# More filler products before the first sums, one fold moved behind a chunk's products, and mask additions moved from VectorE to GpSimd

## The chip, the core and the metric

The kernel runs on one core of one Trainium2 chip. The metric is device time in microseconds (us) from one launch, the median of several runs. The engines are written as in the profile: PE is TensorE's matmul side and PEld its weight loads, DVE is VectorE, ACT is ScalarE, POOL is GpSimd, SP is SyncE, which starts most DMAs. An "ACT table load" is ScalarE fetching another set of functions.

## The reference

Two transformer blocks run one after the other on 256 tokens of width 1024, with 256 context tokens beside them in the first block. What matters here is the first block, which has two layers:

```python
for l in range(DEPTH):                      # DEPTH = 2
    mod_x = silu(c) @ w_ada[l] + b_ada[l]   # nine shifts, scales and gates of 1024
    mod_c = silu(c_ctx) @ w_ada[l] + b_ada[l]
    h  = h  + 0.5*g1 *swiglu(modulate(rms_norm(h),  sh1, sc1), w_gate, w_up, w_down)
    hc = hc + 0.5*cg1*swiglu(modulate(rms_norm(hc), csh1, csc1), w_gate, w_up, w_down)
    p = modulate(rms_norm(h), shm, scm) @ w_in[l]
    ...                                     # window, global and neighbourhood attention
    h = h + gm * (concat(y_w, y_g, y_n) @ w_out[l])
    h = h + 0.5*g2*swiglu(modulate(rms_norm(h), sh2, sc2), w_gate2, w_up2, w_down2)
```

In neighbourhood attention a query sees 4 rows of 16 columns around its own column, with a learned bias for each offset. The kernel scores all 256 keys instead and adds one table to the scores: the learned bias, and a large negative number where a key lies outside the 16 columns. That large negative number is the mask of this change.

## The kernel before

Every product in float32 is made of three matmuls of split operands: each operand is a high part (`..._hi`) and a low part (`..._lo`), and high times high, high times low and low times high are added up in a PSUM bank. ACT makes the high parts with a copy, DVE the low parts with a subtraction. Activations are kept with features on the 128 partitions, in eight chunks `h[:, j, :]` of 512 tokens (256 of x, 256 of the context). The weights come as a stream of panels that SP loads; PE works through them in order. The order on each engine is the order in which the Python program writes its instructions, with semaphores between engines (`Engine.after` waits, `Engine.do` signals).

The opening makes the first norm, the first two shift and scale rows of `mod`, and the first two panels of the first gate and up products at the same time:

- ACT squares the eight chunks and DVE adds them up (L996, L1004). Meanwhile PE runs products of `csil` (silu of the two conditions, 32 columns wide) whose result in bank 0 is never read (L1039): the unread products. Behind them stand the sums over the features by a column of ones (L1054).
- `ada_columns(j)` (L885) multiplies `csil` with the eighth j of the shift and scale columns, on four column groups of PE side by side. `ada_copy(j)` (L898, DVE) copies the result to SBUF, `ada_fold(j)` (L904, PE) adds the four groups up and turns the rows into columns, and `ada_scale(j)` (L913 and L916, DVE) adds the bias. These give chunk j its shift and scale. `columns_begin(j)` is the first two, `columns_end(j)` the last two.
- `norm_scale` spreads the inverse norms over the partitions (L1079, PE). `chunk_hi(j)` multiplies chunk j by them (L1443, DVE), applies scale and shift and makes the high part (L1447, L1450, ACT). `chunk_lo(j)` makes the low part (L1455, DVE). `weights_hi` and `weights_lo` split the weights (L1417, L1427).
- `products(panel, j)` are the matmuls of chunk j (L1488 with the high part of the chunk, L1492 with the low part).

The loop in `opening` writes this for chunk after chunk: while PE multiplies chunk k, DVE and ACT make chunk k+1, and PE takes the columns and the fold for chunk k+2 between `products(0, k)` and the next `products(0, k+1)`.

For the attention of layer l, POOL loads the bias table `nbr` with 12 DMAs as soon as the down panels of the first feed-forward are far enough (L1595). In the phase `in`, which makes queries, keys and values, the norm comes first, and the weight tiles then run between the steps of attention units: a generator `program` gives out weight tiles as filler, and a unit's steps are scores (L1919, PE), `exponentials` (a mask for window heads L1941, a maximum L1942, DVE; L1956, ACT), `normalise` (L1969, L1972, DVE), transposes (L1986, PE), a copy (L1993, ACT), and products with the values (L2008, PE). `turn` is the rotation of queries and keys, whose DVE steps are L1783, L1784 and L1786. After weight tile 8, `nbr_masks` adds the mask to the six heads of `nbr` on DVE (L1796). Neighbourhood units come late in the order, so `nbr` is read late.

In the second layer POOL also loads `vec_2` and the positions behind the bias table, and from the end of the attention on it builds a bias map for the second block in small steps (`bias_map`, L1389 to L1395).

Of the kernel before, what the change touches and what calls it, by code (L numbers as in the profile page):

```python
# [22 lines left out]
P = 128  # L23
# [13 lines left out]
NBR_COLS = 64  # L37
NBR_DR = 2 * NBR_ROWS - 1
# [702 lines left out]
def build(nc, ins, out):  # L741
# [6 lines left out]
    pe, act, dve = e.T, e.A, e.V  # L748
# [41 lines left out]
    def cst(name, width=P, k=0):  # L790
        o = CC.at[name] + k
        if o >= CC.kept:
            return tables[0][:, o - tables[1]:o - tables[1] + width]
        return const[:, o:o + width]
# [38 lines left out]
    loaded = [(s_vec, 16), (s_const, 16)] + [(s, 16) for s in s_tok]  # L833
# [7 lines left out]
    pool = e.G  # L841
# [9 lines left out]
    for l in range(L1):  # L851
        for hh in range(6):
            o = (l * 6 + hh) * NBR_DR
# [181 lines left out]
    dve.after((s_vec, 16))  # L1035
    pe.after((s_vec, 16), c_ready)
    csil_row = csil[:, :, :].rearrange("p k c -> p (k c)")
    for _ in range(9):
        pe.q.matmul(banks[0][0:32, 0:S], csil[:, 0, :], csil_row, start=True, stop=True)  # L1039

    split_u = {}
# [50 lines left out]
    def root_table(function=ACT.Sqrt):  # L1092

        act.do(act.q.activation(root_warm[:, :], cst("eps", 1), function))
# [304 lines left out]
    def opening():  # L1399
# [9 lines left out]
        def columns_end(j):  # L1409

            ada_fold(j)
            scaled_by[j] = ada_scale(j)
# [65 lines left out]
        def products(panel, j):  # L1478

            high, low = chunk[j]  # L1480
            pe.after(weights[j])
            by_stream = j == 0 and panel == 0
            for s in range(2 if by_stream else 1):
                pe.after(high[s] if by_stream else high)
                cols = slice(s * S, s * S + S) if by_stream else slice(0, T)
                for b in range(2):
                    for w in (first_hi, first_lo):
                        pe.q.matmul(banks[2 * panel + b][:, cols], w[:, panel, j, b * P:b * P + P], u_hi[:, j, cols],  # L1488
                                    start=j == 0 and s == 0 and w is first_hi, stop=False)
            pe.after(low)  # L1490
            for b in range(2):
                r = pe.q.matmul(banks[2 * panel + b][:, :], first_hi[:, panel, j, b * P:b * P + P], u_lo[:, j, :],  # L1492
                                start=False, stop=j == KC - 1)
            if j == KC - 1:
                r.then_inc(st.s_pe, 1)
# [14 lines left out]
        weights_lo(1)  # L1510
        columns_begin(2)
        chunk_lo(1)
        columns_end(2)
        weights_hi(2)
        for k in range(1, KC):
            if k == 3:
                root_table(ACT.Silu)
            if k + 1 < KC:
                chunk_hi(k + 1)
                weights_lo(k + 1)  # L1520
                chunk_lo(k + 1)
            if k + 2 < KC:
                weights_hi(k + 2)
            products(0, k)
            if k + 2 < KC:
                columns_begin(k + 2)
            products(1, k - 1)
            if k + 2 < KC:
                columns_end(k + 2)
            if k in (5, 6):  # L1530
                for quarter in (2 * k - 10, 2 * k - 9):
                    st.split_hi(PHASES[0], 2, quarter)
            if k in (6, 7):
                for quarter in (2 * k - 12, 2 * k - 11):
                    st.split_lo(PHASES[0], 2, quarter)
# [5 lines left out]
    for l in range(L1):  # L1541
# [14 lines left out]
        if l == 0:  # L1556
# [11 lines left out]
        nbr = ar.new(f"nbr_bias{l}", [P, 6, NBR_DR + 1, NBR_COLS])  # L1568
# [13 lines left out]
        tab_ready = (s_tab, 16)  # L1582
        s_nbr = nc.alloc_semaphore(f"nbr_bias_loaded{l}")
        pool.q.wait_ge(*rpb_in_dram)
        z = [pool.do(pool.q.memset(nbr[0:64, :, NBR_DR, :], 0.0)),
             pool.do(pool.q.memset(nbr[64:128, :, 0, :], 0.0))]
        pitch = rows * SKEW - 1
        n_nbr = 0
        for half in range(2):
            for hh in range(6):  # L1590
                o = (l * 6 + hh) * NBR_DR * SKEW + NBR_COLS - 1
# [3 lines left out]
                pool.q.dma_start(dst, src).then_inc(s_nbr, 16)  # L1595
                n_nbr += 16
        nbr_loaded = (s_nbr, n_nbr)
        if last:
            pool.q.wait_ge(st.s_ada, L1 * ADA_PANELS)
            pool.q.dma_start(vec_2[:, :], ins["vec_2"]).then_inc(s_vec2, 16)  # L1600
            map_ready = bias_map()
# [8 lines left out]
        at_tile = {x: i for i, x in enumerate(IN_TILES)}  # L1610
        in_first, out_first = PHASE[("in", l)].first, PHASE[("out", l)].first
        sink_ready = dve.do(dve.q.tensor_scalar(neg_sink[:, :], vcol(("sink", l), 0, 6), -1.0, None, ALU.mult))
        evacuated, prepared, bank_free = {}, {}, [None, None]
        jobs_done = [0]

        def next_bank():
# [171 lines left out]
                    prepared[kind, c] = turned[kind, c]  # L1788
            waiting.append(evacuate)

        def nbr_masks():

            dve.after(tab_ready, nbr_loaded, z)
            mask_rows = cst("nbr_mask", NBR_COLS).rearrange("p (o c) -> p o c", o=1)
            for hh in range(6):
                prepared["nbr"] = dve.do(dve.q.tensor_tensor(  # L1796
                    nbr[:, hh, :, :], nbr[:, hh, :, :], mask_rows.to_broadcast([P, NBR_DR + 1, NBR_COLS]), ALU.add))

        y_ready = {}

        def out_tile(i):
# [56 lines left out]
        def program():  # L1858

            yield from first_tiles()  # L1860
            inside = {3: head_sums, 5: lambda: turn("q", 4), 6: lambda: turn("q", 0), 7: lambda: turn("k", 0),
                      8: lambda: v_turn(0), 9: lambda: turn("q", 1), 11: lambda: v_turn(2), 12: lambda: turn("q", 2),
                      15: lambda: v_turn(3)}
            for i in range(2, len(IN_TILES)):
                if i in inside:
                    small.append(inside[i]())
                yield from in_tile(i)
                if i == 4:
                    yield from turn("k", 1)
                    yield from turn("q", 3)  # L1870
                    yield from v_turn(1)
                    yield from key_norm()
                    flush()
                    yield 0
                elif i == 8:
                    nbr_masks()
                    yield 0
            yield from v_turn(4)
            for i in range(16):
                if i == 8:  # L1880
                    flush()
                    yield None
                yield from out_tile(i)
            flush()
# [422 lines left out]
    for c in range(4):  # L2307
        z = pe.q.matmul(banks[c][:, 0:S], wag[0:64, c * P:(c + 1) * P], mix[0:64, 12, :], start=True, stop=True)
    zdone = pe.do(z)
    for c in range(4):  # L2310
        z = pe.q.matmul(banks[4 + c // 2][:, (c % 2) * S:(c % 2 + 1) * S], wag[64:128, c * P:(c + 1) * P], mix[64:128, 12, :], start=True, stop=True)
# [18 lines left out]
    for c in range(4):  # L2330
        z = pe.q.matmul(banks[c][:, 0:S], wag[:, 512 + c * P:512 + (c + 1) * P], mix[:, 13, :], start=True, stop=True)
# [120 lines left out]
    for c in range(4):  # L2452
        z = pe.q.matmul(banks[4 + c // 2][:, (c % 2) * S:(c % 2 + 1) * S], cst("half_ones"), bonus[:, c, :], start=True, stop=True)
# [63 lines left out]
    def products(first_bank, left, right):  # L2517
        for c in range(4):
            for k in range(NCH):
                for hp in range(2):  # L2520
                    z = pe.q.matmul(bank16(first_bank, c, k, hp), part(left, c, k, hp), right(c, k, hp), start=True, stop=True)
        return pe.do(z)
# [651 lines left out]
```

## Time and profile before

| | |
|---|---|
| median of 3 runs | 2337.69 us (2337.11 to 2339.54) |
| the profiled execution, its own time | 2336.8 us |
| its span, first to last instruction | 2335.5 us |
| PE busy | 2263.3 us, 97% of the span |
| DVE busy | 1490.3 us, 64% |
| ACT busy | 962.7 us, 41% |
| POOL busy | 371.8 us, 16% |
| mean granted TensorE clock | 0.986 of full speed |

The time outside the span is 1.3 us in the profiled execution. PE is the engine that is nearly always busy, so a change is worth what it takes from or adds to PE's own time and PE's waits. The ends of matmuls are modelled, so two groups in a timeline can overlap a little; starts are the firmer numbers. The granted clock tells two levels apart: 1.00 is 2.4 GHz and 0.50 is 1.2 GHz. The rows shown below come from the same execution.

### The profile page before, as it was taken

The page shows a single profiled execution, that of the slowest core. Times are in us where ns is not written, and L with a number is a line of the kernel's source. Part 1 is how long each engine was busy: PE and PEld are TensorE (multiplying, and loading weights), DVE is VectorE, ACT ScalarE, POOL GpSimd, SP SyncE. Part 2 cuts the span into 40 slices and gives each one's busy share as a digit, 9 for nine tenths or more (in the row PEclk, how much of TensorE's full clock was granted, in tenths as well). Part 3 has the DMA queues.
Part 4 walks back from the last instruction along what each step waited for, and adds up shares of the span by engine and source line. Part 5 has one row for each costly group of instructions (what it writes and reads, how often), then busy time and mean ns, then how long its engine had stood idle before and what let it go on. Part 6 is the DMA issues. An engine that isn't in the chain of part 4 may idle for free. (4 is left out here: it accounts for less than half of the span.)

```text
span 2335.5 us, 37193 instructions
## 1 busy us (share of the span) xinstructions
PE 2263.3 (97%) x14418; PEld 1923.3 (82%) x14418; DVE 1490.3 (64%) x2318; ACT 962.7 (41%) x1555; POOL 371.8 (16%) x365
## 2 busy tenths in 40 slices
PE   8999999999999999999999999989999999999998
PEld 5888888666678888888888877669998998899998
DVE  5766766565675666666565345656667766777874
ACT  5322223455542222242222244545446434656763
POOL 1000001000000000000000010029997576000000
PEclk9999999999999999999999999999999999999999
DMA  7554445201134444434443242124554332244544
GB/s 279 207 192 173 171 171 173 72 37 55 55 135 162 165 178 175 161 131 172 169 162 137 96 133 90 56 91 153 187 166 174 110 106 73 91 145 163 183 175 147
DMA packets 53911, 331.05 MB, mean 142 GB/s; under 512 B 6688, under 2 KB 7968, under 8 KB 23328
## 3 DMA queue, kind: packets, MB, share of 16 engines
q1 hardware_dynamic: 50336, 319.15, 38.3%
q0 software_dynamic: 3456, 10.25, 1.5%
q8 instruction: 83, 1.36, 0.2%
q14 instruction: 36, 0.29, 0.0%
HBM read 325.56 MB, written 3.80 MB: 141 GB/s over the span
## 5 line engine op out<-in xcount | busy, mean ns | idle before, releaser
L1202 PE MATMUL bank<-u_hi,whi 128*128 128x512 f32 (+1 forms) x2352 | 804.5, 342 | 7.0 <-ACT v L1721 2.6
L1204 PE MATMUL bank<-u_hi,wlo 128*128 128x512 f32 (+1 forms) x2352 | 790.0, 336 | 0.0
L1203 PE MATMUL bank<-u_lo,whi 128*128 128x512 f32 (+1 forms) x2352 | 789.9, 336 | 0.0
L583 DVE TENSOR_TENSOR wlo<-raw,whi 128x2048 fp32r<-128x2048 f32 (+2 forms) x203 | 423.1, 2084 | 304.4 <-ACT whi L581 304.4
L1202 PEld LDWEIGHTS bank<-u_hi,whi 128*128 128x128 f32 x2352 | 443.3, 188 | 66.9 <-issue 9.2
L581 ACT ACTIVATE whi<-raw 128x2048 fp32r<-128x2048 f32 (+2 forms) x203 | 345.5, 1702 | 344.8 <-PE bank L1204 195.8
L1204 PEld LDWEIGHTS bank<-u_hi,wlo 128*128 128x128 f32 x2352 | 443.9, 189 | 47.5
L1203 PEld LDWEIGHTS bank<-u_lo,whi 128*128 128x128 f32 x2352 | 443.3, 188 | 45.2 <-issue 0.2
L1277 ACT ACTIVATE sil<-bank 128x512 f32<-128x512 f32 (+1 forms) x88 | 47.8, 543 | 519.5 <-PE bank L1204 517.1
L1202 PE MATMUL bank<-hidden_hi,whi 128*128 128x512 f32 x528 | 205.4, 389 | 0.0
L1203 PE MATMUL bank<-hidden_lo,whi 128*128 128x512 f32 x528 | 205.4, 389 | 0.0
L1204 PE MATMUL bank<-hidden_hi,wlo 128*128 128x512 f32 x528 | 205.4, 389 | 0.0
L935 DVE SCALAR_TENSOR_TENSOR bank<-raw,c_row 128x1024 f32<-128x1024 f32 x128 | 157.2, 1228 | 8.2 <-DMA raw<-in_stream 7.1
L1395 POOL TENSOR_TENSOR rel_bias_map<-rel_bias_map,bucket_step 128x384 f32<-128x384 f32 x124 | 156.0, 1258 | 10.3
L935 DVE SCALAR_TENSOR_TENSOR raw<-raw,bank 128x1024 f32<-128x1024 f32 x128 | 155.7, 1216 | 0.0
L1581 POOL DMA_DIRECT2D tables<-in_const x2 | 1.1, 574 | 963.6 <-PE bank L1204 963.6
L1281 DVE TENSOR_TENSOR prod<-sil,bank 128x512 f32<-128x512 f32 (+1 forms) x88 | 54.6, 621 | 156.3 <-ACT sil L1277 154.9
L604 DVE TENSOR_TENSOR wlo<-raw,whi 128x1024 fp32r<-128x1024 f32 (+2 forms) x84 | 99.0, 1189 | 81.4 <-ACT whi L596 76.3
L1392 POOL TENSOR_SCALAR bucket_step<-in_bucket,bucket_steps 128x384 f32<-128x384 f32 x124 | 130.8, 1055 | 12.4
L1203 PEld LDWEIGHTS bank<-hidden_lo,whi 128*128 128x128 f32 x528 | 99.1, 188 | 20.7
L1204 PEld LDWEIGHTS bank<-hidden_hi,wlo 128*128 128x128 f32 x528 | 99.1, 188 | 20.6
L1202 PEld LDWEIGHTS bank<-hidden_hi,whi 128*128 128x128 f32 x528 | 99.1, 188 | 20.4
(449 smaller groups left out, 3212.2 us busy)
## 6 DMA issues: line engine op xcount, KB each, us to landing
raw<-in_stream SPq DMA_DIRECT2D x229, 1024.0 KB, 4.8
raw<-in_stream SPq DMA_DIRECT2D x80, 704.0 KB, 4.0
first_ada<-in_stream SPq DMA_DIRECT2D x8, 1024.0 KB, 16.6
raw<-in_stream SPq DMA_DIRECT2D x8, 768.0 KB, 4.4
skew<-rpb_rows POOLq DMA_DIRECT2D x8, 336.0 KB, 6.4
nbr_bias<-skew POOLq DMA_DIRECT2D x24, 112.0 KB, 3.3
h<-in_tokens SPq DMA_DIRECT2D x4, 512.0 KB, 6.4
raw<-in_stream SPq DMA_DIRECT2D x8, 256.0 KB, 16.8
```

What stands on the lines that cost most here:

```text
L581: a.activation(self.hi[to][:, 0:n], raw[:, 0:n], ACT.Copy).then_inc(self.s_hi, 1)
L583: v.tensor_tensor(self.lo[to][:, 0:n], raw[:, 0:n], self.hi[to][:, 0:n].bitcast(F32), ALU.subtract).then_inc(self.s_lo, 1)
L604: r = v.q.tensor_tensor(self.lo[to][:, cols], self.raw[slot][:, cols], self.hi[to][:, cols].bitcast(F32), ALU.subtract)
L935: r = dve.q.scalar_tensor_tensor(out=product, in0=w, scalar=1.0, in1=rows, op0=ALU.mult, op1=ALU.mult, accum_out=to)
L1202: pe.q.matmul(dst, w[0], x[0], start=start, stop=False)
L1203: pe.q.matmul(dst, w[0], x[1], start=False, stop=False)
L1204: return pe.q.matmul(dst, w[1], x[0], start=False, stop=stop)
L1277: act.q.activation(sil[par][:, 0:n], banks[2 * par][:, 0:n], ACT.Silu).then_inc(s_sil, 1)
L1281: dve.q.tensor_tensor(prod[par][:, 0:n], sil[par][:, 0:n], banks[2 * par + 1][:, 0:n], ALU.mult).then_inc(st.s_ev, 1)
L1392: z = pool.do(pool.q.tensor_scalar(step[:, :], bucket[:, :], 1.0 - start, steps[:, hh, b + 1:b + 2], ALU.add, ALU.mult))
L1395: z = pool.do(pool.q.tensor_tensor(rel[:, hh, :], rel[:, hh, :], step[:, :], ALU.add))
L1581: pool.q.dma_start(tab[:, :], ins["const"][:, CC.kept:CC.at["causal"]]).then_inc(s_tab, 16)
```

## The change

Three edits. Seventeen unread products stand ahead of the sums in place of nine. The third fold and its scale (`columns_end(2)`) stand behind the products of chunk 1 with panel 0, and no longer ahead of them. The masks of the neighbourhood bias are added on POOL, right behind its loads, and not on DVE in the middle of the `in` phase.

```diff
-    for _ in range(9):
+    for _ in range(17):
         pe.q.matmul(banks[0][0:32, 0:S], csil[:, 0, :], csil_row, start=True, stop=True)
...
         weights_lo(1)
         columns_begin(2)
         chunk_lo(1)
-        columns_end(2)
         weights_hi(2)
         for k in range(1, KC):
             if k == 3:
                 root_table(ACT.Silu)
+            if k == 1:
+                products(0, 1)
+                columns_end(2)
             if k + 1 < KC:
                 chunk_hi(k + 1)
                 weights_lo(k + 1)
                 chunk_lo(k + 1)
             if k + 2 < KC:
                 weights_hi(k + 2)
-            products(0, k)
+            if k > 1:
+                products(0, k)
             if k + 2 < KC:
                 columns_begin(k + 2)
...
         nbr_loaded = (s_nbr, n_nbr)
+        pool.after(tab_ready, nbr_loaded, z, loaded)
+        mask_rows = cst("nbr_mask", NBR_COLS).rearrange("p (o c) -> p o c", o=1)
+        for hh in range(6):
+            nbr_masked = pool.do(pool.q.tensor_tensor(
+                nbr[:, hh, :, :], nbr[:, hh, :, :], mask_rows.to_broadcast([P, NBR_DR + 1, NBR_COLS]), ALU.add))
+            pool.after(nbr_masked)
...
-        evacuated, prepared, bank_free = {}, {}, [None, None]
+        evacuated, prepared, bank_free = {}, {"nbr": nbr_masked}, [None, None]
...
-        def nbr_masks():
-
-            dve.after(tab_ready, nbr_loaded, z)
-            mask_rows = cst("nbr_mask", NBR_COLS).rearrange("p (o c) -> p o c", o=1)
-            for hh in range(6):
-                prepared["nbr"] = dve.do(dve.q.tensor_tensor(
-                    nbr[:, hh, :, :], nbr[:, hh, :, :], mask_rows.to_broadcast([P, NBR_DR + 1, NBR_COLS]), ALU.add))
...
-                    yield 0
-                elif i == 8:
-                    nbr_masks()
                     yield 0
```

On PE, in the opening, these rows stood from the columns of eighth 2 (`first_ada_56`) to those of eighth 3 (`first_ada_57`). L904 is the fold of eighth 2; L1488 and L1492 are the products of chunk 1 with panel 0.

```order
L885 MATMUL bank<-first_ada_56,csil 32x256 x8
L904 MATMUL bank<-const,inv_norm_diagonal 128x2 x2
L1488 MATMUL bank<-u_hi,first_weights_hi 128x512
L1488 MATMUL bank<-u_hi,first_weights_lo 128x512
L1488 MATMUL bank<-u_hi,first_weights_hi 128x512
L1488 MATMUL bank<-u_hi,first_weights_lo 128x512
L1492 MATMUL bank<-u_lo,first_weights_hi 128x512 x2
L885 MATMUL bank<-first_ada_57,csil 32x256 x8
```

After the change the same place reads as follows.

```order
L885 MATMUL bank<-first_ada_56,csil 32x256 x8
L1488 MATMUL bank<-u_hi,first_weights_hi 128x512
L1488 MATMUL bank<-u_hi,first_weights_lo 128x512
L1488 MATMUL bank<-u_hi,first_weights_hi 128x512
L1488 MATMUL bank<-u_hi,first_weights_lo 128x512
L1492 MATMUL bank<-u_lo,first_weights_hi 128x512 x2
L904 MATMUL bank<-const,inv_norm_diagonal 128x2 x2
L885 MATMUL bank<-first_ada_57,csil 32x256 x8
```

The fold has moved past six matmuls. The rows of DVE and ACT in the opening keep their order, so the scale of eighth 2 (L913) still stands right behind the low part of chunk 1 (L1455) on DVE.

On POOL, in the second layer, the rows from the tables' load to the positions' were these, with the semaphores that they wait for.

```order
L1581 DMA tables_8277<-in_const 128x1088 [waits panel_multiplied]
L1585 MEMSET nbr_bias_8278 64x6x64 [waits rpb_moved]
L1586 MEMSET nbr_bias_8278 64x6x64
L1595 DMA nbr_bias_8278<-skew 64x7x64 x12
L1600 DMA vec_49<-in_vec 128x646 [waits ada_panel_multiplied]
```

After the change the same place reads as follows.

```order
L1584 DMA tables_8299<-in_const 128x1088 [waits panel_multiplied]
L1588 MEMSET nbr_bias_8300 64x6x64 [waits rpb_moved]
L1589 MEMSET nbr_bias_8300 64x6x64
L1598 DMA nbr_bias_8300<-skew 64x7x64 x12
L1604 TENSOR_TENSOR nbr_bias_8300<-nbr_bias_8300,tables_8299 128x512 [waits pool_done,nbr_bias_loaded1,tables_loaded1]
L1604 TENSOR_TENSOR nbr_bias_8300<-nbr_bias_8300,tables_8299 128x512 [waits pool_done] x5
L1609 DMA vec_49<-in_vec 128x646 [waits ada_panel_multiplied,pool_done]
```

Six additions now stand behind the bias loads, and the load of `vec_2` waits for them. On DVE the six additions of each layer are gone; apart from these places the order on every engine is as it was.

## Rows read from the trace of the kernel before

**Rows 1.** The page: span, and PE's busy time, share and instructions.
```profile
span 2335.5 us, 37193 instructions
...
PE 2263.3 (97%) x14418; PEld 1923.3 (82%) x14418; DVE 1490.3 (64%) x2318; ACT 962.7 (41%) x1555; POOL 371.8 (16%) x365
```
**Rows 2.** Windows of the opening: stretch, PE busy, granted clock, DMA share, GB/s.
```profile
8.00:12.30 4.30, 0.83 (x4) 1.00 1.02 418
...
14.00:21.00 7.00, 7.00 (x46) 0.50 1.02 415
...
24.00:27.00 3.00, 2.01 (x25) 1.00 1.05 421
```
**Rows 3.** Timeline of PE in the opening: start, duration, group, idle before and releaser.
```profile
3.32 5.51 PE L1039 MATMUL bank<-csil 128*32 128x256 f32 x18 [3.32 <-ACT csil L871]
12.36 1.21 PE L1054 MATMUL bank<-const,ssq 128*128 128x1 f32 x8 [3.53 <-DVE ssq L1004]
...
18.94 0.85 PE L904 MATMUL bank<-const,inv_norm_diagonal 128*128 128x2 f32 x4
...
21.84 0.58 PE L1488 MATMUL bank<-u_hi,first_weights_hi 128*128 128x256 f32 x1 [0.19 <-DVE first_weights_lo L1427]
...
23.57 0.63 PE L1492 MATMUL bank<-u_lo,first_weights_hi 128*128 128x512 f32 x2
24.04 0.50 PE L904 MATMUL bank<-const,inv_norm_diagonal 128*128 128x2 f32 x4
...
26.53 0.61 PE L904 MATMUL bank<-const,inv_norm_diagonal 128*128 128x2 f32 x4 [0.99 <-DVE inv_norm_diagonal L898]
27.47 0.47 PE L1488 MATMUL bank<-u_hi,first_weights_hi 128*128 128x512 f32 x1 [0.34 <-ACT u_hi L1450]
...
29.02 1.07 PE L885 MATMUL bank<-first_ada,csil 128*32 128x256 f32 x16
```
**Rows 4.** Timeline of PE's weight loads, the last ten passes of the unread products.
```profile
6.28 2.07 PEld L1039 LDWEIGHTS bank<-csil 128*32 128x32 f32 x10 [0.25 <-issue]
```
**Rows 5.** Timeline of PE in layer 0's second norm: the same sums and spread.
```profile
395.13 0.95 PE L1054 MATMUL bank<-const,ssq 128*128 128x1 f32 x8
...
396.38 1.05 PE L1054 MATMUL bank<-const,prod 128*128 128x1 f32 x8 [0.30 <-ACT prod L1021]
...
397.54 1.16 PE L1079 MATMUL bank<-const,inv_norm 128*128 128x128 f32 x8
```
**Rows 6.** Windows of the same norm, columns as in rows 2.
```profile
399.00:405.00 6.00, 5.40 (x17) 0.50 0.75 174
```
**Rows 7.** Timeline of DVE: low part of chunk 1, bias of eighth 2.
```profile
27.36 0.69 DVE L1455 TENSOR_TENSOR u_lo<-sil,u_hi 128x512 fp32r<-128x512 f32 x1 [0.88 <-ACT u_hi L1450]
27.96 0.16 DVE L913 TENSOR_TENSOR mod<-bank,vec 128x4 f32<-128x4 f32 x1
```
**Rows 8.** Waits of PE's weight loads, 28 to 52 us: total, times, longest.
```profile
PEld bank L904 <- DVE inv_norm_diagonal L898: 1.5, 5, 0.6
```
**Rows 9.** Timeline around the masks of layer 1, all engines.
```profile
1455.12 3.69 DVE L1796 TENSOR_TENSOR nbr_bias<-nbr_bias,tables 128x512 f32<-128x512 f32 x6
...
1460.07 1.13 PE L1919 MATMUL bank<-kT,qT 64*128 64x512 f32 x4 [0.33 <-DVE qT L1786]
...
1461.83 0.60 ACT L1993 ACTIVATE probs_t<-bank 128x512 f32<-128x512 f32 x1 [6.04 <-PE bank L1986]
...
1463.53 0.66 PE L1986 MATMUL bank<-const,probs 128*128 128x128 f32 x4 [1.74 <-DVE probs L1972]
...
```
**Rows 10.** Timeline of POOL in layer 1: the loads of the bias table.
```profile
1385.91 8.68 POOL L1595 DMA_DIRECT2D nbr_bias<-skew  x12
```
**Rows 11.** Groups by line: POOL, whole span; busy us, mean ns, idle before.
```profile
L1395 POOL TENSOR_TENSOR rel_bias_map<-rel_bias_map,bucket_step 128x384 f32<-128x384 f32 x124 | 156.0, 1258 | 10.3
```
**Rows 12.** Groups by line: DVE, 1380 to 1404 us, no POOL arithmetic beside it.
```profile
L637 DVE TENSOR_TENSOR wlo<-raw,whi 128x512 fp32r<-128x512 f32 x4 | 2.7, 684 | 0.0
```
**Rows 13.** Groups by line: DVE, 1560 to 1600 us, while POOL builds its map.
```profile
L637 DVE TENSOR_TENSOR wlo<-raw,whi 128x512 fp32r<-128x512 f32 x4 | 3.9, 987 | 0.0
```

## The prediction

> **What bounds the kernel now.** I read the page first: PE is busy 2263.3 of 2335.5 us, 97% of the span [rows 1]. So time can come only from PE's 72 us of idle time or from stretches where PE works slowly. I then looked where the three edits stand, since the rest of the program keeps its order on every engine. The windows of the opening show the granted clock at 1.00 until 12.3 us, at 0.50 from 14 to 21 us and at 1.00 again from 24 us [rows 2]. The timeline of PE says what PE did before the clock fell: the unread products ran from 3.32 to 8.83 us, and then PE sat idle for 3.53 us until the last square was added [rows 3]. A stage that PE runs at half clock, on a chain where each engine waits for the other, is the first thing this change touches. The second is the chain of chunks 1 and 2 in the same opening, the third is the attention of the two layers.
>
> **Seventeen products.** The weight loads show ten passes of the unread products in 2.07 us, the later ones, which is 0.21 us for a pass and 0.41 for a product of two passes [rows 4]. The first eight of the 18 passes took the other 3.44 of 5.51 us [rows 3], 0.43 each or 0.86 for a product, so PE was still at its slower pace there. Eight more products at the later pace take 8 x 0.41 = 3.3 us, so they end at 8.83 + 3.3 = 12.1 us. The sums start at 12.36 us because DVE's last addition ends then [rows 3]. So the products themselves cost nothing, the cover is the squares on ACT and DVE, and the idle time of PE is gone. Without this cover they would cost their 3.3 us. If the pace rises later in an execution than in this one, more of the products take twice as long: with four more at 0.86 us the end moves by 1.8 us to 13.9 us, and the sums are 1.5 us late.
>
> What is it worth if the clock stays at 1.00? From the start of the sums, 12.36, to the end of the first fold, 18.94 + 0.85 = 19.79 us, the chain takes 7.43 us at the low clock [rows 3]. The same steps at the high clock stand elsewhere: the two sums take 0.95 and 1.05 us and the spread 1.16 us in layer 0's second norm [rows 5], the columns 1.07 us and a fold 0.50 us later in the opening [rows 3]. Their sum is 4.73 us, so the fold is done 2.7 us earlier. DVE and ACT then make chunk 0 in a time that the clock doesn't touch. Its eight short matmuls run from 21.84 to 23.57 us, at the low clock nearly to the end, 1.7 us [rows 3], and would take 0.9; the low part of the chunk from DVE then comes last, which leaves about 0.7 of the 0.8 us. Together 3.4 us, the start of the second fold moving from 24.04 to 20.6 us. The bounds are 0, if the clock falls all the same, and 3.6 us, if DVE hides the whole difference.
>
> **The third fold.** In the rows of before it stands at 26.53 us, in an idle time of PE (0.99 us ahead of it, 0.34 us behind it), and the products of chunk 1 start at 27.47 because ACT's high part comes then, not because of the fold [rows 3]. So moving it frees nothing on PE. It does delay DVE: the bias of eighth 2 stands right behind the low part of chunk 1 and runs at 27.96 us with no wait [rows 7]. Behind the products, the fold starts when these end, at 29.02 us by the place where the next columns start, takes 0.50 us [rows 3], and the bias follows at about 29.6 us. That is 1.6 us later. Queued behind it on DVE are the scaled chunk 2, the split of weights 2, the low part of chunk 2 and the copy for the fourth fold; ACT waits for the first, PE for the last. Is there slack that takes this up? From 28 us on PE's weight load for a fold waits for DVE's copy in each of the 5 rounds, 1.5 us in all [rows 8]. The round is set by DVE and ACT, and PE already waits a little in each, so nothing is caught up: +1.6 us. All these places move with the gain above and keep their distances. The lower bound is 0, if something else holds chunk 2 up; above, 1.6 + 0.5, if the fold itself is added to PE's round.
>
> **The masks.** In layer 1 the six additions hold DVE for 3.69 us at 1455 us. PE waits 0.33 us for the rotation behind them at 1460.07 and 1.74 us for probabilities at 1463.53 [rows 9]. The upper bound of the gain is their sum, 2.1 us. What is late next? ACT copies the transposed unit at 1461.83, behind the scores at 1460.07, and makes the exponentials only then; the next scores need these [rows 9]. With DVE free, that copy moves up only by the 0.33 us of the rotation, and so do the exponentials and the scores behind them. So I take 0.4 us, near the lower end. In layer 0 I take 0, since no wait of PE there ends on the masks or on what directly follows them. The edit gives nothing away on POOL's queue: `vec_2` and the positions, which were loaded right behind the bias table at 1394.6 us [rows 10], come some 10 us later, and the first to read them is the bias map, at work only in the stretch from 1560 us [rows 13].
>
> What the additions cost on POOL: its addition of 384 columns takes 1258 ns on average [rows 11], so 512 columns take 1.7 us (an estimate, by the ratio), six 10 us. They start when the last bias load has landed, a few us behind its issue at 1394.6 us [rows 10], while the norm of that layer is still in its last chunks, and in layer 0 likewise. There DVE splits weights and chunks from two SBUF operands. The same split takes 684 ns without POOL arithmetic beside it and 987 ns with it [rows 12, 13], 0.3 us more for each. Some four such steps meet the masks in layer 1 and three in layer 0; PE waits for one or two chains of these in layer 1 and hardly for one in layer 0. I take +0.5 us in all. The lower bound is 0; above, all seven at 0.3 us, 2.1 us.
>
> The Trainium skill's page "SBUF — State Buffer", section "SBUF: two separate sides", says that the ports which VectorE and GpSimd share are an exclusive lock: a VectorE instruction with two SBUF inputs waits until a GpSimd instruction that reads SBUF is through, and the other way round. The rows agree in direction, 684 against 987 ns [rows 12, 13], but show a mean far below a whole POOL instruction. By the rule at its worst the sum would be 2344 us in place of 2336.0; that is the last rival, worked out below from rows.
>
> **The sum.** -3.4 + 1.6 - 0.4 + 0.5 = -1.7 us. The profiled execution took 2336.8 us, its span 2335.5 us and 1.3 us around it; it would become 2335.1 us. The median of the runs is 2337.7 us, 0.9 above it, so for the median I forecast 2336.0 us. This is 0.07%, and about 0.2% (4.7 us) is what a measurement of this kernel can tell from no change.
>
> **The rivals.**
>
> The clock falls again (2338.4 us). For it speaks the second norm of layer 0: PE comes to the sums from a stage of dense products, the sums are short and come with waits, and the clock is at 0.50 from 399 to 405 us [rows 5, 6]. In the opening the columns stand between sums and spread, which is more work, but afterwards PE idles ahead of chunk 1, 1.3 us in two pieces now [rows 3], and 2 us or more once it gets there early and the fold no longer breaks the gap. If it falls there, PE runs some 6 us of dense products at half clock as in rows 6, which costs up to 3 us, and if it falls at the sums, the whole 3.4 us is lost: 2336.0 + 2.4 between these, up to 2339.4 us. Against it: the gap in front of the sums, which is what the clock fell behind, is closed.
>
> The fold costs nothing and DVE's freedom pays in full (2332.1 us): -3.4 + 0 - 2.1 = -5.5 us from 2337.7. It needs chunk 2 to be held up by something other than DVE's queue, and ACT to follow DVE in layer 1. The rows speak against both, but half of it would already give 2334 us.
>
> The added products come too late (2337.5 us): the pace rises later than here, they outlast the squares by 1.5 us as worked out above, and this eats most of the gain. For it: eight of 18 passes were slow in this execution, and nothing in the program fixes that number. Against it: even then the squares cover most of the added work.
>
> The port decides (2344 us). If each of the seven DVE steps, and the next POOL addition in turn, waits out a whole instruction of 1.7 us on a chain that PE waits for, 7 x 1.7 = 12 us less what is off PE's path, some 4 us, come on top of 2336.0. It decides from about four full waits on, 6.4 us. Against it: the four splits in rows 13 lost 0.3 us each on average, beside POOL at work.
>
> **How the numbers follow.** The forecast's own case has 0.46, with a range of its own from 2334.4 us, with the fold at 0, to 2337.6 us, with POOL's cost at 2.1. The clock that falls again has 0.30, the full gain 0.10, the late products 0.08, the port 0.06. The likeliest case gives 2336.0 us. The range from 2332.8 to 2340.4 us takes in all but the tail of the full gain and the port, and leaves room of 1 us for the median to lie elsewhere among the runs. Faster by over 0.2% means below 2333.0 us: the full gain, 0.10. Slower means above 2342.4 us: the port, 0.06. The rest, 0.84, is within.
>
> **What would show it.** In the timeline of PE, 34 passes of L1039 that end close to 12.2 us, and no idle time ahead of the sums; the windows from 13 to 21 us at a clock of 1.00; the second fold near 20.6 us. The bias of eighth 2 on DVE should wait for PE by over a microsecond, and the fourth fold come only about 1.8 us earlier than before, half of what the second gains. POOL should show six additions of 1.4 to 1.7 us from about 1398 us, and DVE's splits beside them longer than 684 ns; PE's wait of 1.74 us near 1463 us should shrink but leave others in its place. The prediction is wrong if the clock stays at 0.50 in those windows, if the fourth fold has gained as much as the second, or if DVE loses more than a microsecond to any single POOL addition.

## Result and profile after

The changed kernel takes 2347.1 us (median of 6 runs, 2344.5 to 2349.0), the kernel before 2338.7 us in the same series: 1.0037 times as long, with a 95% interval of 1.0027 to 1.0047, or some 8.7 us more (8.4 by the medians). The profiled execution took 2347.0 us. That is outside the predicted range, on its slow side, and it is the case of the last rival, the port, to which the prediction gave a chance of 0.06.

The page of the changed kernel, its span and busy times, against [rows 1]:

```profile
span 2345.7 us, 37233 instructions
...
PE 2267.6 (97%) x14434; PEld 1925.0 (82%) x14434; DVE 1494.8 (64%) x2306; ACT 962.7 (41%) x1555; POOL 389.6 (17%) x377
```

DVE has 12 instructions less and is busy 4.5 us longer, although 7.4 us of mask additions have left it. POOL has 12 more and is busy 17.8 us longer. In the six profiles with the masks on DVE and no added work on POOL, DVE is busy for 1489.4 to 1494.3 us, so the sum alone proves little; busy time that grows on the engine that was to be relieved is a first sign.

**The opening.** The timeline of PE, against [rows 3]:

```profile
3.39 9.56 PE L1039 MATMUL bank<-csil 128*32 128x256 f32 x34 [3.39 <-ACT csil L871]
12.88 1.05 PE L1054 MATMUL bank<-const,ssq 128*128 128x1 f32 x8
...
21.00 0.50 PE L904 MATMUL bank<-const,inv_norm_diagonal 128*128 128x2 f32 x4
...
24.43 0.57 PE L1488 MATMUL bank<-u_hi,first_weights_hi 128*128 128x512 f32 x1 [1.93 <-ACT u_hi L1450]
...
26.93 0.85 PE L904 MATMUL bank<-const,inv_norm_diagonal 128*128 128x2 f32 x4
...
31.68 0.61 PE L904 MATMUL bank<-const,inv_norm_diagonal 128*128 128x2 f32 x4 [1.17 <-DVE inv_norm_diagonal L898]
...
57.56 0.50 PE L1202 MATMUL bank<-u_hi,whi 128*128 128x512 f32 x1
```

And windows of it, columns as in [rows 2]:

```profile
14.00:21.00 7.00, 5.96 (x63) 1.00 1.02 416
...
25.00:28.00 3.00, 3.00 (x13) 0.50 1.04 421
```

The 34 passes run up to the sums and the clock stays at 1.00 through sums, spread and first fold. They end at 12.95 us, 0.6 us behind DVE's last square (12.32 us), so the sums start 0.5 us later than before. The second fold is 3.0 us earlier than in [rows 3]. But without the fold in between, PE idles 1.93 us in one piece ahead of chunk 1, and the clock falls to 0.50 there. The fourth fold, at 31.68 us, has gained 0.14 us on the kernel before:

```profile
31.82 0.61 PE L904 MATMUL bank<-const,inv_norm_diagonal 128*128 128x2 f32 x4
```

**The masks in layer 0.** The timeline of all engines at the end of the norm ahead of the attention:

```profile
408.18 9.16 POOL L1604 TENSOR_TENSOR nbr_bias<-nbr_bias,tables 128x512 f32<-128x512 f32 x6 [2.62 <-issue]
...
408.53 1.49 DVE L1170 TENSOR_TENSOR u_lo<-sil,u_hi 128x512 fp32r<-128x512 f32 x1
...
409.94 1.77 DVE L637 TENSOR_TENSOR wlo<-raw,whi 128x512 fp32r<-128x512 f32 x1
...
411.63 0.68 DVE L1135 TENSOR_TENSOR prod<-h,bank 128x512 f32<-128x512 f32 x1
...
412.23 2.30 DVE L1154 SCALAR_TENSOR_TENSOR u_lo<-sil,mod,u_hi 128x256 fp32r<-128x256 f32 x2
...
414.45 1.76 DVE L1170 TENSOR_TENSOR u_lo<-sil,u_hi 128x512 fp32r<-128x512 f32 x1
...
414.58 1.22 PE L1233 MATMUL bank<-u_lo,whi 128*128 128x512 f32 x2 [2.87 <-DVE u_lo L1154]
...
416.14 1.76 DVE L637 TENSOR_TENSOR wlo<-raw,whi 128x512 fp32r<-128x512 f32 x1
```

Read the durations on DVE. A split of 128x512 takes 0.68 us alone [rows 12]; here it takes 1.77 and 1.76. Each step with both operands in SBUF (L1170, L637, L1154) stands beside one POOL addition. Taken one by one, the four steps of 128x512 end 0.54 or 0.55 us after the addition beside them, and the two of 128x256 in L1154 0.28 us after it: they do most of their own work only when the addition is over. The step of the same size that reads one operand from PSUM (L1135, `h,bank`) takes its usual 0.68 us in the middle of them. PE then waits 2.87 us for one low part. Layer 1 shows the same: six additions in 9.16 us from 1401.50 us, splits of 1.77 us, and a wait of PE of 3.18 us at 1407.89 us.

Behind the waits the clock falls. Windows of PE in both layers (PE busy, granted clock, DMA share, GB/s):

```profile
408.00:414.00 6.00, 3.38 (x13) 0.98 0.00 0
414.00:420.50 6.50, 5.08 (x11) 0.50 0.23 49
1401.00:1407.00 6.00, 3.35 (x16) 1.00 0.00 0
1407.00:1413.80 6.80, 5.38 (x19) 0.50 0.24 73
```

PE had waited 2.87 and 3.18 us in one piece just before, and then works at the lower of its two levels, 1.2 GHz, through the rest of the norm and into the first tile. In the kernel before, the clock is at 1.00 from 407 to 420.5 us and from 1400 to 1416 us. What it costs is read on ACT, which takes each finished tile from its bank. Two such steps, first in the kernel before, then in the changed kernel:

```profile
413.90 0.60 ACT L1698 ACTIVATE prod<-bank 128x512 f32<-128x512 f32 x1 [1.54 <-PE bank L1233]
...
420.89 0.60 ACT L1698 ACTIVATE prod<-bank 128x512 f32<-128x512 f32 x1 [2.86 <-PE bank L1204]
```

```profile
417.98 0.60 ACT L1707 ACTIVATE prod<-bank 128x512 f32<-128x512 f32 x1 [3.88 <-PE bank L1233]
...
427.23 0.60 ACT L1707 ACTIVATE prod<-bank 128x512 f32<-128x512 f32 x1 [5.13 <-PE bank L1204]
```

The tile behind the norm takes 6.99 us before and 9.25 us after: 2.3 us for the clock, on top of the 4.1 us by which its beginning is late. ACT's 1555 steps come in the same order in both kernels, so each can be set against its like. They are 6.3 us late at this tile, but only 4.7 us from 430 us on, because the kernel before has a fall of the clock of its own there (0.50 from 426.2 to 429.5 us) where the changed kernel runs at 1.00. In layer 1 the same two steps are 8.0 and 10.5 us late, against 4.8 us in the chunks before them. So this profile loses 4.9 us in layer 0 and 5.9 us in layer 1.

**DVE's freedom.** The place where the masks stood in layer 1, against [rows 9]:

```profile
1470.42 1.13 PE L1917 MATMUL bank<-kT,qT 64*128 64x512 f32 x4
...
1472.17 0.60 ACT L1991 ACTIVATE probs_t<-bank 128x512 f32<-128x512 f32 x1 [5.62 <-PE bank L1984]
...
1472.91 0.63 PE L1984 MATMUL bank<-const,probs 128*128 128x128 f32 x4 [0.78 <-ACT probs_t L1991]
...
1474.16 1.13 PE L1917 MATMUL bank<-kT,qT 64*128 64x512 f32 x4 [0.61 <-ACT probs L1954]
```

The wait for the rotation is gone and the wait of 1.74 us has become 0.78; the next scores then wait 0.61 us for ACT. ACT's copy at 1472.17 us comes 1.75 us behind the scores, against 1.76 us in [rows 9], and ACT's wait ahead of it falls from 6.04 to 5.62 us, so the unit moves up by 0.4 us.

### The profile page after: what moved, and what is told of

Same layout as the page of the kernel before. It is cut to its first block and busy times, and to the rows that moved or that the text cites. A ratio compares the mean times of both kernels' runs of the same rounds, so it can differ in the third digit from the quotient of the medians.

```text
span 2345.7 us, 37233 instructions
## 1 busy us (share of the span) xinstructions
PE 2267.6 (97%) x14434; PEld 1925.0 (82%) x14434; DVE 1494.8 (64%) x2306; ACT 962.7 (41%) x1555; POOL 389.6 (17%) x377
## 5 line engine op out<-in xcount | busy, mean ns | idle before, releaser
L1202 PE MATMUL bank<-u_hi,whi 128*128 128x512 f32 (+1 forms) x2352 | 805.2, 342 | 7.3 <-ACT v L1730 2.6
L1202 PEld LDWEIGHTS bank<-u_hi,whi 128*128 128x128 f32 x2352 | 443.9, 189 | 67.9 <-issue 9.2
L1202 PE MATMUL bank<-hidden_hi,whi 128*128 128x512 f32 x528 | 205.4, 389 | 0.0
L1395 POOL TENSOR_TENSOR rel_bias_map<-rel_bias_map,bucket_step 128x384 f32<-128x384 f32 x124 | 157.5, 1270 | 10.3
L1392 POOL TENSOR_SCALAR bucket_step<-in_bucket,bucket_steps 128x384 f32<-128x384 f32 x124 | 130.5, 1052 | 12.4
L1202 PEld LDWEIGHTS bank<-hidden_hi,whi 128*128 128x128 f32 x528 | 99.1, 188 | 20.4
```

The costliest lines, as they stand in the source:

```text
L1202: pe.q.matmul(dst, w[0], x[0], start=start, stop=False)
L1392: z = pool.do(pool.q.tensor_scalar(step[:, :], bucket[:, :], 1.0 - start, steps[:, hh, b + 1:b + 2], ALU.add, ALU.mult))
L1395: z = pool.do(pool.q.tensor_tensor(rel[:, hh, :], rel[:, hh, :], step[:, :], ALU.add))
```

## Experiments

The theory after the two traces: a DVE step with both operands in SBUF waits for the POOL addition that is running, for nearly its whole length; five such waits in a row in the last chunks of the norm, and the fall of the clock behind them, are the loss. The rival: the opening's edits, or POOL's work as such, or chance in the clock.

**1. The masks on POOL alone** (the third edit as in the diff above, the opening as before).

> The kernel before with the third edit alone (masks added on POOL, behind the bias loads). Theory A, POOL's additions hold up DVE in the norm ahead of the attention: nearly all of the loss is here, +6 to +10 us against the kernel before, with five DVE steps of 1.5 to 1.8 us in a row in each layer where they took 0.69. Rival B, the edits of the opening are the cause and the falls of the clock in the norms only chance: within 2 us of the kernel before.

Measured: 2345.0 us against 2338.6, ratio 1.0028 (1.0018 to 1.0037), some 6.5 us. DVE's steps of 128x512 in its profile between 406 and 420 us (group by line: busy us, mean ns):

```profile
L637 DVE TENSOR_TENSOR wlo<-raw,whi 128x512 fp32r<-128x512 f32 x2 | 3.5, 1774 | 0.0
L1170 DVE TENSOR_TENSOR u_lo<-sil,u_hi 128x512 fp32r<-128x512 f32 x3 | 3.2, 1070 | 0.5 <-ACT u_hi L1165 0.4
```

The clock falls behind these steps here too, to 0.51 from 414 to 420.5 us and to 0.53 from 1407 to 1413.8 us. So by the medians some three quarters of the loss is this edit.

**2. The opening's two edits alone.**

> The kernel before with the two edits of the opening alone (seventeen unread products, third fold behind a chunk's products). Theory A: between -2.5 and +1 us; the changed kernel's trace shows 0.14 us gained by the opening's end, since the clock falls again at 24.65 us. Rival B: +6 to +9 us, with a loss that comes later than the opening.

Measured: 2339.8 us against 2338.6, ratio 1.0006 (0.9998 to 1.0015), about +1.4 us and not told apart from nothing. Its opening ends at 57.65 us, with the clock down at 26.05 us behind the same idle time of 1.93 us. Theory A's range for it reached to +1: the sign of the opening's sum is in doubt from here on.

**3. Seventeen products alone, twice.**

```diff
-    for _ in range(9):
+    for _ in range(17):
```

> Seventeen unread products alone, the third fold in its old place. If the late fold gave the gain back: -3 to -1 us, the fourth fold some 1.5 us earlier than in the changed kernel (30.2 us instead of 31.7). If the second fall of the clock gave it back: 0 to -0.5 us, the clock at 0.50 again from about 24 us on and the fourth fold near 31.7 us.

> Seventeen unread products alone once more, for its median and a second profile of its opening. The first profile had the opening end 2.7 us earlier than the mean of six profiles of the old one (53.87 against 56.6 us), its median gained nothing. If that profile was a lucky one: the clock falls to 0.50 between 21 and 28 us here and the opening ends near 56 us. If the gain is usual: it ends near 54 us, and the median lies 1 to 3 us under the kernel before.

Measured: ratios 1.0002 (0.9990 to 1.0014) and 1.0002 (0.9992 to 1.0012). The end of the opening (first L1202 on PE) in the two profiles:

```profile
53.87 0.50 PE L1202 MATMUL bank<-u_hi,whi 128*128 128x512 f32 x1
```

```profile
55.86 0.50 PE L1202 MATMUL bank<-u_hi,whi 128*128 128x512 f32 x1
```

In the first the clock stays at 1.00 to the end, in the second it falls at 24.75 us behind an idle time of 0.99 us. Seven profiles of kernels with the old opening end it between 55.48 and 57.70 us, 56.4 on average; the profile of before, from which I had worked, is the slowest of the seven. A gain of 0.5 to 2.5 us in the opening is left, and the medians do not show it. In the first profile the fourth fold comes at 28.00 us, earlier than in either case of the first expectation, and still the median gained nothing; the second profile is its lucky-profile case.

**4. The late fold alone.** (`columns_end(2)` moved behind `products(0, 1)`, as in the diff above.)

> The third fold behind the products of chunk 1, alone. My step: +1.6 us, the opening (start of the following phase on PE) at 58 to 59.5 us where three profiles of the old opening show 56.5 to 57.7. Rival: nothing, since the clock's rises in the opening shift by as much as this.

Measured: ratio 1.0002 (0.9993 to 1.0011). The opening ends at 58.74 us, later than any of the seven old ones, and the clock falls behind PE's 1.93 us ahead of chunk 1. The price of the step is seen in the profile; the median can't tell it from nothing.

**5. No masks at all**, on either engine.

> The kernel before without the mask additions on any engine, so keys outside the 16 columns count in neighbourhood attention: what freeing DVE of its 3.7 us a layer is worth. My step says -0.4 us (the next units wait for ACT's copy), the upper bound was -2.1 us. A gain beyond 2 us would say that the additions on POOL cost more than the result shows.

The kernel leaves the mask out, so its output is not the reference's. Measured: ratio 0.9999 (0.9989 to 1.0010). The median can't show the 0.4 us expected, but the profiles do. Against the kernel before, ACT's copy at that place and the steps behind it move up by 0.40 to 0.43 us here and in the six other profiles in which DVE does not add the masks, and by at most 0.03 us in the six profiles in which it does.

**6. The additions in smaller pieces**, in the same place on POOL (here in quarters; halves with 4 rows each).

```diff
+            for r in range(0, NBR_DR + 1, 2):
-                nbr[:, hh, :, :], nbr[:, hh, :, :], mask_rows.to_broadcast([P, NBR_DR + 1, NBR_COLS]), ALU.add))
+                    nbr[:, hh, r:r + 2, :], nbr[:, hh, r:r + 2, :], mask_rows.to_broadcast([P, 2, NBR_COLS]), ALU.add))
```

> Masks on POOL in the norm, each of the six additions of 512 columns cut into four of 128. Theory A (a DVE step waits for the one POOL instruction that is running): the 1.76 us steps of DVE fall to 0.9 to 1.2 us, and the loss from +6.5 to between +1 and +4 us. Rival B (the two engines share the port by its bandwidth): POOL moves the same bytes, so DVE loses as much in all, +5 to +8 us.

> Masks on POOL in the norm, each addition cut into two of 256 columns: between whole additions (+6.5 us) and quarters (no change). Theory A, a DVE step waits for the POOL instruction that is running, so the loss goes with the length of one instruction: DVE's steps of 0.69 us at 1.1 to 1.4 us, +1 to +4 us. Rival, only the number of bytes or a fixed threshold counts: +6 us again, or nothing with steps under 1 us.

Measured: quarters 1.0002 (0.9992 to 1.0011), halves 0.9999 (0.9989 to 1.0010): the loss is gone in both. DVE's split (406 to 420 us) and POOL's addition (403 to 422 us) by line in the quarters, then in the halves:

```profile
L637 DVE TENSOR_TENSOR wlo<-raw,whi 128x512 fp32r<-128x512 f32 x2 | 1.9, 944 | 0.0
...
L1602 POOL TENSOR_TENSOR nbr_bias<-nbr_bias,tables 128x128 f32<-128x128 f32 x24 | 14.2, 592 | 4.3 <-issue 2.4
```

```profile
L637 DVE TENSOR_TENSOR wlo<-raw,whi 128x512 fp32r<-128x512 f32 x2 | 2.5, 1230 | 0.0
...
L1602 POOL TENSOR_TENSOR nbr_bias<-nbr_bias,tables 128x256 f32<-128x256 f32 x12 | 12.4, 1034 | 3.0 <-issue 2.2
```

The wait of a split is 0.26, 0.55 and 1.08 us for pieces of 128, 256 and 512 columns (944, 1230 and, in the changed kernel, 1762 ns, less 684). It doubles with the columns of POOL's instruction, while the bytes that POOL moves in all are the same: DVE waits for the one instruction that is running, and the two engines do not share by bytes. My expectations of a loss in between, for the halves and for the quarters, fell. In the halves the waits do halve, but PE's wait for a low part is 0.7 us in place of 2.9 in layer 0, and 1.55 in place of 3.18 in layer 1, and the clock does not fall behind either (1.00 from 407 to 420.5 us and from 1400 to 1416 us). Up to the last low part of layer 0's norm, DVE's steps lose 4.4 us in all beside whole additions, 1.0 beside halves and 0.7 beside quarters; ACT's steps behind it lose 4.2, 0.5 and 0.4 us. So short waits go in part into slack of the chain, and long ones come out nearly whole, with the clock's fall on top.

**7. Other work on POOL in that place**, masks on DVE as before.

```diff
+            if last:
+                work_done = pool.do(pool.q.tensor_scalar(pbuf[1][:, :, :], pbuf[0][:, :, :], 1.0, None, ALU.mult))
+            else:
+                work_done = pool.do(pool.q.memset(pbuf[1][:, :, :], 0.0))
```

> Masks on DVE as before, and at the place where the third edit put the additions POOL does other work: in layer 0 nine zeroings of a tile (writes only), in layer 1 one zeroing and eight products of a tile with a number (one SBUF operand read). Theory A, what holds DVE up is a POOL instruction that reads SBUF: no DVE step over 0.9 us in layer 0, steps of 1.4 to 1.8 us in layer 1, +2 to +5 us in all. Rival B, any POOL instruction beside DVE does it: long steps in both layers, +5 to +8 us. Rival C, only a POOL instruction with two SBUF operands does: no long steps, within 1.5 us of the kernel before.

Measured: ratio 1.0018 (1.0008 to 1.0028), some 4 us. Timeline of POOL and DVE, layer 0 (writes only), then layer 1 (one operand read):

```profile
407.76 6.02 POOL L1605 MEMSET probs<- 128x1024 f32 x6
407.80 0.68 DVE L637 TENSOR_TENSOR wlo<-raw,whi 128x512 fp32r<-128x512 f32 x1
...
410.91 0.69 DVE L1170 TENSOR_TENSOR u_lo<-sil,u_hi 128x512 fp32r<-128x512 f32 x1 [1.03 <-ACT u_hi L1165]
...
412.78 1.02 DVE L1620 TENSOR_SCALAR neg_sink<-vec 128x6 f32<-128x6 f32 x1
```

```profile
1396.36 2.87 POOL L1603 TENSOR_SCALAR probs<-probs 128x1024 f32<-128x1024 f32 x1
1396.51 1.52 DVE L637 TENSOR_TENSOR wlo<-raw,whi 128x512 fp32r<-128x512 f32 x1
```

Writes alone leave the splits at 0.68 us, and ACT's steps in layer 0 lose nothing, so busy POOL is not the cause; a POOL instruction that reads SBUF is. In layer 1 the split loses 0.84 us and is through at 1398.03 us, 1.2 us before POOL's instruction ends. The splits at 1400.45 and 1401.06 us, 1.1 and 1.8 us into the next product, lose nothing (0.69 and 0.68 us). So theory A held in kind, but there POOL held DVE up for its first microsecond only. By ACT's steps layer 1's norm loses 1.9 us, with the clock at 0.72 from 1401 to 1407 us; the rest of the 4 us is not located.

The Trainium skill's page "SBUF — State Buffer", section "SBUF: two separate sides", has a DVE instruction with two SBUF inputs locked out by a GpSimd instruction that reads SBUF, for the whole of that instruction. The additions (1.08 us of wait beside 1.29 us of POOL) and the zeroings agree with it; the products of 2.8 us, which let DVE through after about 1 us, do not, and there the measurement decides. The same section of the Trainium skill has a DVE instruction in a mode that takes both ports wait for any GpSimd instruction; the 1.02 us of the small step at 412.78 us, 0.17 in the changed kernel, is in line with it, though no run shows the mode.

**8. The masks on POOL later**, beside the attention.

```diff
+        pool.q.wait_ge(st.s_pe, PHASE[("in", l)].first + 5)
```

> Masks on POOL as in the third edit, but POOL first waits until the fifth panel of the attention's input weights is multiplied, so the six additions miss the norm and come beside the splits and rotations of the attention. Theory A (the place of the collision matters, since in the norm PE waits for each DVE step): within 2 us of the kernel before. Rival B (POOL's additions cost the same wherever they stand): +5 to +8 us as with the masks in the norm (+6.5).

Measured: ratio 1.0036 (1.0022 to 1.0049), 7.5 us: theory A's half of this fell, the place did not save it. The timeline in layer 1:

```profile
1462.89 8.10 POOL L1602 TENSOR_TENSOR nbr_bias<-nbr_bias,tables 128x512 f32<-128x512 f32 x6 [65.33 <-PE bank L1204]
...
1464.29 1.23 DVE L1964 TENSOR_TENSOR stat<-stat 128x2 f32<-128x2 f32 x1
...
1465.75 2.77 DVE L1968 TENSOR_SCALAR probs<-probs,stat 128x512 f32<-128x512 f32 x2
...
1468.58 0.66 PE L1982 MATMUL bank<-const,probs 128*128 128x128 f32 x4 [4.13 <-DVE probs L1968]
```

An addition of two columns, 0.16 us of work, takes 1.23 us, and the two scalings 2.77 us where they take 0.88. The scalings read one tensor and a column of factors, so the wait is not confined to steps with two full operands; the theory's words were too narrow there. The steps between scores and transposes are all on PE's path: PE waits 4.13 us for the probabilities, against 1.74 in [rows 9].

**9. Seventeen products with the idle times behind them filled** by two unread products each, ahead of chunk 0 and of the third fold.

```diff
+        unread_products(2)
         products(0, 0)
...
+        unread_products(2)
         columns_end(2)
```

> Seventeen unread products, the fold in its old place, and two more unread products each in the idle times of PE ahead of chunk 0 and ahead of the third fold (1.05 and 0.99 us idle). If falls of the clock behind these idle times take the gain of the seventeen back: the clock stays at 1.00 from the sums on, the opening ends near 54 us, -2 to -4 us against the kernel before. If not: within 1 us of seventeen alone.

Measured: ratio 0.9999 (0.9991 to 1.0008). The clock is at 1.00 in its profile from 13 to 28 us, and the opening ends at 55.25 us because the sums start at 13.47 us: the pace of the first products rose late in this execution. No gain that the median shows, with the two idle times filled and no fall of the clock in the opening.

**10. All three edits, the additions in quarters.**

> The changed kernel with all three edits, and each mask addition on POOL cut into four of 128 columns. If the length of one POOL instruction is what made the change slower, only the loss of the two opening edits is left: 0 to +2 us against the kernel before, no DVE step over 1.0 us in the norm's last chunks, and no fall of the clock behind them. If something else in the combination adds to it: +4 us or more.

Measured: ratio 1.0001 (0.9992 to 1.0011), where the change as it stands gives 1.0037. The split takes 948 ns. With the one thing altered that the theory names, the loss is gone. No version here is measurably faster than the kernel before.

## Why the prediction was wrong

**The step that failed is the price of POOL's additions**, "0.3 us more for each ... I take +0.5 us in all", with 2.1 us as its upper bound. Alone this edit costs some 6.5 us, 4 to 9 by its interval. A step loses up to 1.1 us, not 0.3, which is the prediction's own sign of being wrong ("more than a microsecond to any single POOL addition"). Five places in a row lose in each layer, and PE waits 2.9 and 3.2 us. The 0.3 came from a mean [rows 13]. The four splits in it, one by one in the trace of before, with the POOL instructions beside the second and the last of them:

```profile
1573.88 1.09 DVE L637 TENSOR_TENSOR wlo<-raw,whi 128x512 fp32r<-128x512 f32 x1
...
1580.85 1.42 POOL L1392 TENSOR_SCALAR bucket_step<-in_bucket,bucket_steps 128x384 f32<-128x384 f32 x1
1581.22 0.68 DVE L637 TENSOR_TENSOR wlo<-raw,whi 128x512 fp32r<-128x512 f32 x1
...
1583.82 0.68 DVE L637 TENSOR_TENSOR wlo<-raw,whi 128x512 fp32r<-128x512 f32 x1
1584.96 1.41 POOL L1395 TENSOR_TENSOR rel_bias_map<-rel_bias_map,bucket_step 128x384 f32<-128x384 f32 x1
1585.42 1.50 DVE L637 TENSOR_TENSOR wlo<-raw,whi 128x512 fp32r<-128x512 f32 x1
```

Two splits lost nothing: they stood beside POOL's L1392, which reads one tensor. Two lost 0.4 and 0.8 us; the last came with 0.95 us of an addition left and ended 0.55 us after it. The mean of 987 ns is that of steps that met an addition and steps that did not, and where six additions stand end to end nearly every step meets one. The row was at hand before the prediction, and the argument against the port, that rows 13 show "a mean far below a whole POOL instruction", was a wrong reading of it.

**The clock behind the waits** was in no term; by ACT's rows it costs 2.3 us in layer 0, of which 1.6 us come back when the kernel before has its own fall. That the fall belongs to the waits is shown only so far: it came in both layers of both profiles with whole additions in the norm, and in neither layer of the three with pieces.

**The port's rival** named the mechanism, the steps and the condition, "from about four full waits on", and its 2344 us is 3 us short of the result. That it comes so near is in part luck: it had seven waits of 1.7 us, where the trace has up to 1.1 us at ten places, and no fall of the clock, and it stood on an opening that gains 1.8 us. What was most wrong was its chance.

**Seventeen products:** the mechanism was right (no idle time ahead of the sums, clock at 1.00, second fold 3.0 us earlier against 3.4), the size was not. The term was taken from one execution whose opening was the slowest of seven; against their mean the two profiles of seventeen products alone gain 0.5 and 2.5 us. The step "the products themselves cost nothing" failed by a little: in all six profiles with seventeen products they outlast DVE's last square, by 0.2 to 2.1 us, since their pace rises later than in the one execution of before or the squares are done sooner. So the rival of the late products, with its 0.08, came true in part in all of them. The rival in which the clock falls again came true in the changed kernel, at the place named, the gap ahead of chunk 1. **The third fold:** predicted +1.6 us, 2.3 us later than the mean of the old openings in its own profile. Part of it is that without the fold PE's idle time ahead of chunk 1 is in one piece, which the prediction had noted under the rival and not under the fold. Together the two edits are at +1.4 us (-0.5 to +3.5) and not at -1.8.

**DVE's freedom:** predicted 0.4 us in layer 1 and 0 in layer 0. This term was right, with its reason: in all seven profiles without masks on DVE at that place ACT's copy moves up by 0.40 to 0.43 us in layer 1, and nothing moves at the same place in layer 0. The medians alone, good to 2.6 us, could not have shown it. One slip of the sums changes nothing: the full gain is 2337.7 - 5.5 = 2332.2 us, not 2332.1.

What stays open: why 0.5 to 2.5 us of the opening do not appear in the medians of seventeen products. Executions of one kernel differ by over 10 us here (2330.6 to 2342.3 us), and the narrower of the two intervals still allows a gain of 1.9 us. In the first profile of seventeen products ACT's steps lead the kernel before by 3.8 us behind the opening and by 4.1 us at 1460 us, and are 0.1 us late at the end: what they lose, they lose in stretches that this edit doesn't touch. It is also open why the norms of the two layers lose 10.8 us in the profile of the changed kernel, and 10.3 us in that of the masks on POOL alone, where the medians differ by 8.7 and 6.5 us.

## What to carry to other kernels

Before work is moved from VectorE to GpSimd, list the VectorE steps that will run beside it, those with two SBUF operands above all, and price each at a whole GpSimd instruction; if the work has to go there, cut it into short instructions. When a mean is to price a collision, look at the single instructions behind it: a mean of 0.3 us may be two waits of nothing and two of 0.4 and 0.8 us. And a term that rests on where the clock fell in one profile wants a second profile before it is a size.

## What the runs showed of the hardware

Cutting POOL's additions into quarters made POOL's own time longer (14.2 us in place of 8.8 in layer 0) and the kernel 6 us faster. Waits of DVE of up to 0.55 us left no trace in the median, waits of 1.08 us cost 6.5 us. POOL pays as well: its addition of 512 columns takes 1.29 us when no held-up DVE step is at work as it starts, and up to 1.62 us when one is. And a POOL instruction that reads one operand of 1024 columns held DVE up in its first microsecond only, out of 2.8.
